# Expert down weights loaded as neighbouring rows, with a stepped product on VectorE to match

## The chip, the cores and the metric

The kernel runs on one core of a Trainium2 chip. The metric is the device time of one execution in microseconds (us), and a kernel's time is the median of its runs. The profile is of one further execution, taken by the hardware profiler.

## What is computed

A two-layer trunk over one sequence of 256 tokens with 1024 channels, in float32: a convolution module and a dense SwiGLU, then shared keys and values, a windowed attention and a mixture of experts, then a final norm. The change lies in the experts. The reference for them, shortened:

```python
D_FF_EXPERT, N_EXPERTS, TOP_K = 3584, 8, 2

def swiglu(t, w_gate, w_up, w_down):
    return (jax.nn.silu(t @ w_gate) * (t @ w_up)) @ w_down

def moe_swiglu(h, router_w, router_b, w_gate, w_up, w_down):
    ...
    out = jnp.zeros_like(t)
    for e in range(N_EXPERTS):
        out = out + combine[:, e:e + 1] * swiglu(t, w_gate[e], w_up[e], w_down[e])
    return out.reshape(B, S, D)
```

The product with `w_down` is a sum over the 3584 hidden channels. Any order of these channels gives the same sum, as long as the activations and the rows of `w_down` are in the same order.

## The kernel before, in words

**The expert stage.** The kernel makes one pass for each expert (and one more for each expert with over 128 tokens; here there are eight passes in all). A pass gathers up to 128 tokens of the expert and goes through the 3584 hidden channels in seven blocks of 512 (`EB`). For each block it computes the gate product, the up product and the down product, each as three float32r matmuls in place of one float32 matmul: every weight and every activation is split into a high part (`wh`, `ath`) and a low part (`wl`, `atl`), and high by high, low by high and high by low are summed in PSUM (`three_passes`, whose matmuls the profile shows at L992).

**Units and halves.** Weights come in units of 1 MB, 8 KB in each of the 128 partitions. A block has six: two each for gate, up and down (`expert_units`, line 89). A gate or up unit holds 512 columns of four rows for each partition, so pieces of 2 KB. A down unit holds two whole rows of `w_down` (1024 floats, 4 KB) for each partition; row k of a block's four row groups is at channel 128 k + p for partition p (line 454), so the two rows of one partition lie 512 KB apart. Each unit is split in two halves. ScalarE copies a half to its high part (`high_parts`, L687), VectorE subtracts it to get the low part (`low_parts`, L1428), and six matmuls of TensorE use it.

**Buffers.** The raw units lie in a ring of seven (`RING`), the split halves in four places (`SPLITS`). SP issues the load of a unit when VectorE has split the unit seven before it (line 461). ScalarE writes a high part when TensorE has used the half four before it.

**One block, in the order of each queue.** All orders are written out by hand.
- TensorE (`expert_pass`, line 1259): gate of block b, the transposes of block b-1's activations, up of block b, down of block b-1. After the last block it transposes the last activations, gathers the next pass's tokens, does the down product, and begins the next pass's gate product.
- ScalarE (line 829): the silu of the gate product into the tile `act` (L823), the high part of the transposed activations (L827), and the high halves of the weights in the order of use.
- VectorE (line 1695): low halves of the gate and up weights, the low part of the transposed activations (`act_low`, L1679), low halves of the previous block's down weights, and then `gate_up` (line 1682, the product at L1686): `act` is multiplied by the up product in PSUM bank 1. The result goes back into `act`. In block 3 of every pass `slots(i + 1)` comes right behind it (lines 1708 to 1711): it loads two registers and makes four selection tiles for the next pass (`pick_slots`, L1632 and L1636).
- TensorE's `transpose_act` (line 1240, L1243) waits for that product and turns its four chunks of 128 channels (`act[:, j * P:(j + 1) * P]`) into four stationary tiles, chunk j against row group j of the block's down weights in `expert_out`.

R3 is a float32 tile of 128x3136; `act` is its first 512 columns and appears as `R` in the profile.

Of the kernel before, what the change touches and what calls it, by code (L numbers as in the profile page):

```python
# [20 lines left out]
P = 128  # L21
# [47 lines left out]
ALU = mybir.AluOpType  # L69
# [19 lines left out]
def expert_units():  # L89

    order = [("g", 0), ("u", 0)]
    for b in range(1, EB):
        order += [("g", b), ("u", b), ("d", b - 1)]
    order.append(("d", EB - 1))
    return [(kind, b, part) for kind, b in order for part in range(2)]
# [18 lines left out]
def trunk(nc, x, norm_mix_g, norm_ffn_g, conv_pw1_w, conv_pw1_b, conv_dw_w, conv_dw_b, conv_ln_g,  # L114
# [4 lines left out]
    with ctx:  # L119
        def sb(name, shape, dt=F32):  # L120
            return ctx.enter_context(nc.sbuf_tensor(name, shape, dt))

        def sem(name):
            return ctx.enter_context(nc.semaphore(name))
# [26 lines left out]
        R3 = sb("R3", [P, 3136])  # L151
        ident = sb("ident", [P, P])
# [12 lines left out]
        PB = [ctx.enter_context(nc.psum_tensor(f"bank{b}", [P, HALF], F32)) for b in range(8)]  # L165
# [46 lines left out]
        hnh = high[:, CHUNK:CHUNK + TT * D].rearrange("p (t d) -> p t d", t=TT)  # L212
        hrT = R2[:, 0:2048].rearrange("p (k s) -> p k s", k=DC)
        act = R3[:, 0:512]
        pickg = R3[:, 1280:1536].rearrange("p (t s) -> p t s", t=TT)
        iota = R3[:, 2816:3072]
        tri = R3[:, 2368:2496]
# [117 lines left out]
        act_ready = sem("act_ready")  # L335
# [8 lines left out]
        def slot(n):  # L344
            return ring[:, n % RING, :]
# [10 lines left out]
        def product_done(eng, n, later=0):  # L356

            if n < U_FFD:
                eng.wait_ge(units_used, n + 1)
            else:  # L360
                eng.wait_ge(halves_used, later * PASS_HALVES + half_no(n, 1) + 1)
# [11 lines left out]
        def split_done(eng, n, h, later=0):  # L373

            eng.wait_ge(wl_ready, later * PASS_HALVES + half_no(n, h) + 1)
# [4 lines left out]
        def tokens(ap, t):  # L380
            return ap[..., t * P:(t + 1) * P]

        def x_bank(t, half):
            return PB[2 * t + half]
# [21 lines left out]
        def _(sp):  # L406
# [44 lines left out]

            mg = moe_w_gate[0].rearrange("e (k p) f -> e p k f", p=P)
            mu = moe_w_up[0].rearrange("e (k p) f -> e p k f", p=P)
            md = moe_w_down[0].rearrange("e (k p) f -> e p k f", p=P)

            def load_pass(i, e):

                for u, (kind, b, part) in enumerate(expert_units()):
                    n = U_MOE + u

                    split_done(sp, n - RING, 1, i)
                    if kind == "d":
                        dst = slot(n).rearrange("p (k f) -> p k f", k=2)
                        src = md[bass.ds(e, 1), :, 4 * b + 2 * part:4 * b + 2 * part + 2, :]
                    else:
                        dst = slot(n).rearrange("p (k f) -> p k f", k=4)
                        src = (mg if kind == "g" else mu)[bass.ds(e, 1), :, 4 * part:4 * part + 4,
                                                          HALF * b:HALF * (b + 1)]
                    sp.dma_start(dst, src.rearrange("e p k f -> p (e k) f")).then_inc(slot_in[n % RING], 16)


            load_pass(0, 0)
            with sp.Fori(1, E) as e:
                load_pass(e, e)
# [3 lines left out]
            with sp.If(passes > E):  # L478
                with sp.Fori(E, passes) as i:
                    e = sp.value_load(tab[0:1, bass.ds(i, 1)], min_val=0, max_val=E - 1)  # L480
                    load_pass(i, e)
# [397 lines left out]
        def _(pe):  # L879
# [34 lines left out]
            for c in range(DC):  # L914
                mm = pe.transpose(PB[3][:, 32 * c:32 * c + CONV], rows[32:32 + CONV, c * P:(c + 1) * P],
                                  ident[32:32 + CONV, 32:32 + CONV])
# [3 lines left out]
            for j in range(4):  # L920
# [4 lines left out]
                for g in range(2):  # L925
# [6 lines left out]
                    for c in range(2):  # L932
                        for k in range(DC):
                            if n == 0 and c == 0:
                                h_ready(0, k)
                            mm = pe.matmul(PB[2 * g + j % 2][:, c * S:(c + 1) * S], w[:, k, c * P:(c + 1) * P],  # L936
                                           hT[:, k, :], start=(k == 0), stop=(k == DC - 1))
# [12 lines left out]
            for m, (c, w) in enumerate(matrix_taps()):  # L950

                pe.wait_ge(tap_act, m + 1)
                if w == 0:
                    pe.wait_ge(glu_ready, c + 1)
                last_tap = SHARED_TAPS - 1 if c == DVE_CHUNKS else CONV - 1
                mm = pe.matmul(PB[4 + c - DVE_CHUNKS][:, 0:S], taps[:, m % DIAGS, :], upad[:, c, w:w + S],  # L956
                               start=(w == 0), stop=(w == last_tap))
# [6 lines left out]
            for t in range(TT):  # L964
                for c in range(DC):
                    pe.wait_ge(sq_ready, 2 * t + (1 if c < DVE_CHUNKS else 2))
                    mm = pe.matmul(PB[3 - t][:, 0:P], ones[:, :], tokens(sq[:, c, :], t), start=(c == 0),  # L967
                                   stop=(c == DC - 1))
# [3 lines left out]
            for t in range(TT):  # L972
                for k in range(DC):
# [4 lines left out]
                    for half in range(2):  # L978
                        mm = pe.matmul(x_bank(t, half)[:, :], tokens(sq[:, k, :], t),  # L979
                                       w[:, k % 2, half * HALF:(half + 1) * HALF], start=(k == 0),  # L980
                                       stop=(k == DC - 1))
# [7 lines left out]
            def three_passes(out_bank, a, b, start, stop, **kw):  # L989

                for n, (lhs, rhs) in enumerate(((a[0], b[0]), (a[1], b[0]), (a[0], b[1]))):
                    mm = pe.matmul(out_bank, lhs, rhs, start=start and n == 0, stop=stop and n == 2, **kw)  # L992
                return mm

            def parts(n, h, cols):

                return wh[:, place(n, h), cols], wl[:, place(n, h), cols]
# [76 lines left out]
            for t in range(TT):  # L1074
                for k in range(DC):
                    if t == 0 and k % 4 == 0:
                        split_done(pe, U_KV + 1, k // 4)
                    mm = three_passes(PB[1][:, t * S:(t + 1) * S], (tokens(hTh[:, k, :], t), tokens(hTl[:, k, :], t)),
                                      parts(U_KV + 1, k // 4, slice(k % 4 * S, (k % 4 + 1) * S)),
                                      k == 0, k == DC - 1)  # L1080
# [79 lines left out]
            for t in range(TT):  # L1160

                pe.wait_ge(x_upd, B_X + 2 * (t + 1))
                for k in range(DC):
                    mm = pe.transpose(PB[4 + 2 * t + k // 4][:, k % 4 * P:(k % 4 + 1) * P], X[:, t, k * P:(k + 1) * P],
                                      ident[:, :])
# [4 lines left out]
            for t in range(TT):  # L1170
                pe.wait_ge(hrT_act, t + 1)
                pe.wait_ge(hrT_dve, t + 1)
                for k in range(DC):
                    mm = pe.matmul(PB[t][:, 0:E], hrT[:, k, t * P:(t + 1) * P], rw[:, k, :],
                                   start=(k == 0), stop=(k == DC - 1))
# [64 lines left out]
            def transpose_act(i, b):  # L1240
                pe.wait_ge(act_ready, i * EB + (b + 1))
                for j in range(4):
                    mm = pe.transpose(PB[2][:, j * P:(j + 1) * P], act[:, j * P:(j + 1) * P], ident[:, :])  # L1243
                mm.then_inc(actT_done, 1)

            def combine(i, t, banks=(5, 6)):
# [12 lines left out]
            def expert_pass(i, last):  # L1259

                pe.wait_ge(gates_ready, i + 1)
                for t in range(TT):

                    pe.matmul(PB[7][:, S:S + 1], pickg[:, t, :], ones[:, 0:1], start=(t == 0), stop=(t == TT - 1))
                for t in range(TT):
                    mm = pe.transpose(PB[7][:, t * P:(t + 1) * P], pick[:, t, :].bitcast(F32), ident[:, :])
                mm.then_inc(place_done, 1)
                for b in range(1, EB):
                    expert_in(i, "g", b)
                    transpose_act(i, b - 1)  # L1270
                    expert_in(i, "u", b)
                    expert_out(i, b - 1)
                transpose_act(i, EB - 1)
                gather(i + 1)
                expert_out(i, EB - 1, (0,))
                gather_T(i + 1)
                expert_out(i, EB - 1, (1,))

                if not last:
                    expert_in(i + 1, "g", 0)  # L1280
                combine(i, 0)
                if not last:
                    expert_in(i + 1, "u", 0)
                    combine(i, 1)
                else:
                    combine(i, 1, (0, 1))
# [19 lines left out]
        def _(ve):  # L1306
# [375 lines left out]
            def gate_up(i, b):  # L1682

                ve.wait_ge(sil_ready, i * EB + (b + 1))
                product_done(ve, expert_at["u", b, 1], i)
                ve.tensor_tensor(act, PB[1][:, :], act, ALU.mult).then_inc(act_ready, 1)  # L1686

            def add_share(i, t, banks=(5, 6)):

# [5 lines left out]
            def expert_pass(i, last):  # L1695

                gate_up(i, 0)
                split_low(i, "u", 1)
                act_low(i, 0)
                split_low(i, "d", 0)  # L1700
                gate_up(i, 1)
                for b in range(2, EB):
                    split_low(i, "g", b)
                    split_low(i, "u", b)
                    act_low(i, b - 1)
                    split_low(i, "d", b - 1)
                    gate_up(i, b)
                    if b == 3:

                        ve.wait_ge(place_done, i + 1)  # L1710
                        slots(i + 1)
# [81 lines left out]
```

## Time and profile before

| | |
|---|---|
| median of 3 runs | 1433.01 us (1430.46 to 1433.05) |
| the profiled execution: its time | 1430.62 us |
| its span, from the first to the last instruction | 1428.9 us |
| TensorE (PE) busy | 1406.5 us, 98% |
| VectorE (DVE) busy | 1170.0 us, 82% |
| ScalarE (ACT) busy | 990.4 us, 69% |
| GpSimd (POOL) busy | 35.8 us, 3% |
| granted TensorE clock | 0.997 of full speed |
| moved by DMA | 417.47 MB, 292 GB/s over the span |

Busy times of one engine are shares of the same span, so they don't add up over engines. PEld is TensorE's weight load, which runs beside its matmuls. A matmul's end is modelled: two that follow each other overlap in the profile, so their pace is read from their starts or from the chain. The idle time of an engine that isn't the bottleneck costs nothing by itself.

### The profile page before, as it was taken

How to read it: one execution, taken by the hardware profiler on the slowest of the kernel's cores; microseconds unless marked ns; L12 is line 12 of the kernel's file. 1: busy time of each engine (PE TensorE's matmuls, PEld its weight loads, DVE VectorE, ACT ScalarE, POOL GpSimd, SP SyncE). 2: the span in 40 equal slices, each digit the busy share in tenths (PEclk: the TensorE clock that was granted, in tenths of full speed). 3: DMA queues.
4: the chain of work that ended last, by engine and by line, in shares of the span. 5: the costliest groups of instructions: out<-in, count | busy, mean ns of one | idle time of the engine just before them, and what ended most of it. 6: DMA issues, size and time to landing. Idle time of an engine off the chain costs nothing.

```text
span 1428.9 us, 21427 instructions
## 1 busy us (share of the span) xinstructions
PE 1406.5 (98%) x7251; PEld 1185.9 (83%) x7251; DVE 1170.0 (82%) x1340; ACT 990.4 (69%) x1224; POOL 35.8 (3%) x62
## 2 busy tenths in 40 slices
PE   9999999999999999999999999999999999999997
PEld 8885999998887888888888888888888888888885
DVE  3983454456769998998999899899989989999996
ACT  2174434445657888887888888787888888878775
POOL 1000000002220000000000000000000000000000
PEclk9999999999999999999999999999999999999999
DMA  9602655655528999999999899999989999998991
GB/s 293 209 28 91 204 177 182 197 181 177 178 89 295 366 381 322 373 360 345 359 363 380 313 382 360 342 363 366 382 311 377 366 328 369 356 390 319 373 364 76
DMA packets 194063, 417.47 MB, mean 292 GB/s; under 512 B 6911, under 2 KB 43903, under 8 KB 194014
## 3 DMA queue, kind: packets, MB, share of 16 engines
q1 hardware_dynamic: 192510, 412.79, 80.6%
q0 software_dynamic: 1344, 3.98, 1.2%
q8 instruction: 31, 0.51, 0.1%
q14 instruction: 18, 0.15, 0.0%
q10 hardware_dynamic: 160, 0.04, 0.0%
HBM read 414.95 MB, written 1.84 MB: 292 GB/s over the span
## 4 chain that ended last, share of the span: by engine, by line
PE 94%; DVE 2%; ACT 2%; issue 1%; POOL 1%; DMA 0%; DVEq 0%; POOLq 0%; ACTq 0%
PE bank L992 78%; PE bank L936 4%; PE bank L956 2%; PE bank L979 2%; PE bank L1243 2%; PE bank L891 1%; PE bank L1194 1%; PE bank L1255 1%; DVE wl L1428 1%; ACT wh L687 1%; PE bank L903 0%; ACT low L812 0%; POOL prob L567 0%; PE bank L1205 0%; PE bank L967 0%
## 5 line engine op out<-in xcount | busy, mean ns | idle before, releaser
L1428 DVE TENSOR_TENSOR wl<-ring,wh 128x1024 fp32r<-128x1024 f32 x758 | 905.8, 1221 | 115.1 <-ACT wh L687 75.8
L687 ACT CAST wh<-ring 128x1024 fp32r<-128x1024 f32 x758 | 787.8, 1054 | 187.7 <-PE bank L992 187.6
L992 PE MATMUL bank<-wh,low 128*128 128x512 f32 (+1 forms) x1840 | 576.1, 392 | 3.4 <-DVE wl L1428 2.8
L992 PEld LDWEIGHTS bank<-wh,low 128*128 128x128 f32 x1840 | 339.6, 188 | 75.9 <-DVE wl L1428 8.7
L992 PE MATMUL bank<-wl,low 128*128 128x512 f32 x896 | 349.7, 390 | 0.0
L992 PE MATMUL bank<-wh,ath 128*128 128x512 f32 x528 | 206.3, 391 | 0.0
L992 PE MATMUL bank<-wh,atl 128*128 128x512 f32 x528 | 205.6, 389 | 0.0
L992 PE MATMUL bank<-wl,ath 128*128 128x512 f32 x528 | 205.5, 389 | 0.0
L992 PEld LDWEIGHTS bank<-wl,low 128*128 128x128 f32 x896 | 168.2, 188 | 36.0
L992 PEld LDWEIGHTS bank<-wl,ath 128*128 128x128 f32 x528 | 99.1, 188 | 20.8
L992 PEld LDWEIGHTS bank<-wh,ath 128*128 128x128 f32 x528 | 99.2, 188 | 20.2
L992 PEld LDWEIGHTS bank<-wh,atl 128*128 128x128 f32 x528 | 99.2, 188 | 19.9
L992 PE MATMUL bank<-high,wh 128*128 128x256 f32 x368 | 104.3, 283 | 0.7 <-DVE low L1439 0.7
L992 PE MATMUL bank<-low,wh 128*128 128x256 f32 x368 | 104.1, 283 | 0.0
L992 PE MATMUL bank<-high,wl 128*128 128x256 f32 x368 | 104.1, 283 | 0.0
L992 PEld LDWEIGHTS bank<-high,wh 128*128 128x128 f32 x368 | 70.6, 192 | 1.4 <-DVE low L1439 0.7
L992 PEld LDWEIGHTS bank<-high,wl 128*128 128x128 f32 x368 | 70.6, 192 | 0.4
L992 PEld LDWEIGHTS bank<-low,wh 128*128 128x128 f32 x368 | 70.6, 192 | 0.0
L1377 DVE SCALAR_TENSOR_TENSOR R<-R 128x256 f32<-128x256 f32 x169 | 67.4, 476 | 0.0
L936 PE MATMUL bank<-R,ring 128*128 128x256 f32 x256 | 55.5, 379 | 0.0
L936 PEld LDWEIGHTS bank<-R,ring 128*128 128x128 f32 x256 | 48.6, 190 | 6.9 <-issue 0.3
L1679 DVE TENSOR_TENSOR atl<-bank,ath 128x512 fp32r<-128x512 f32 x56 | 38.3, 684 | 10.5 <-ACT ath L827 10.5
(213 smaller groups left out, 998.8 us busy)
## 6 DMA issues: line engine op xcount, KB each, us to landing
ring<-in_moe_w_gate SPq DMA_DIRECT2D x112, 1024.0 KB, 5.9
ring<-in_moe_w_up SPq DMA_DIRECT2D x112, 1024.0 KB, 6.3
ring<-in_moe_w_down SPq DMA_DIRECT2D x112, 1024.0 KB, 6.3
ring<-in_conv_pw_w SPq DMA_DIRECT2D x12, 1024.0 KB, 11.2
ring<-in_ffd_w_gate SPq DMA_DIRECT2D x11, 1024.0 KB, 5.4
ring<-in_ffd_w_up SPq DMA_DIRECT2D x11, 1024.0 KB, 5.3
ring<-in_ffd_w_down SPq DMA_DIRECT2D x11, 1024.0 KB, 4.9
ring<-in_w_q SPq DMA_DIRECT2D x4, 1024.0 KB, 4.9
```

The source lines that it names most:

```text
L687: sa.copy(wh[:, place(n, h), :], ring_half(n, h)).then_inc(wh_ready, 1)
L891: pe.matmul(PB[bank][:, 0:P], ident[:, :], ident[:, :], start=True, stop=True)
L936: mm = pe.matmul(PB[2 * g + j % 2][:, c * S:(c + 1) * S], w[:, k, c * P:(c + 1) * P], hT[:, k, :], start=(k == 0), stop=(k == DC - 1))
L956: mm = pe.matmul(PB[4 + c - DVE_CHUNKS][:, 0:S], taps[:, m % DIAGS, :], upad[:, c, w:w + S], start=(w == 0), stop=(w == last_tap))
L979: mm = pe.matmul(x_bank(t, half)[:, :], tokens(sq[:, k, :], t), w[:, k % 2, half * HALF:(half + 1) * HALF], start=(k == 0), stop=(k == DC ...
L992: mm = pe.matmul(out_bank, lhs, rhs, start=start and n == 0, stop=stop and n == 2, **kw)
L1194: mm = pe.matmul(PB[5 + half][:, :], pick[:, t, :], part[:, t, half * HALF:(half + 1) * HALF], start=(t == 0 and n == 0), stop=(t == 1 and ...
L1243: mm = pe.transpose(PB[2][:, j * P:(j + 1) * P], act[:, j * P:(j + 1) * P], ident[:, :])
L1255: mm = pe.matmul(PB[banks[half]][:, :], placeT[:, t * P:(t + 1) * P], part[:, half * HALF:(half + 1) * HALF], start=(n == 0), stop=(n == 1))
L1377: ins = ve.scalar_tensor_tensor(out=v, in0=upad[:, c, w:w + S], scalar=dw[:, c, w:w + 1], in1=v, op0=ALU.mult, op1=ALU.add)
L1428: ve.tensor_tensor(wl[:, place(n, h), :], ring_half(n, h), wh[:, place(n, h), :].bitcast(F32), ALU.subtract).then_inc(wl_ready, 1)
L1679: ve.tensor_tensor(atl[:, :, :], PB[2][:, :].rearrange("p (j s) -> p j s", j=4), ath[:, :, :].bitcast(F32), ALU.subtract).then_inc(atl_rea ...
```

## The change

The load of a down unit views the down weights of a block as channel 4 p + k for partition p and row group k. The four rows of one partition are then neighbours in memory, 16 KB in one piece, and a unit takes half of them, 8 KB in one piece. To match, the activation of channel 4 q + j has to be element q of chunk j. VectorE's product puts it there: it reads both inputs with a step of four floats and writes each chunk in a row, into a new tile `act_by`, columns 512 to 1023 of R3. The transposes read `act_by`.

```diff
         act = R3[:, 0:512]
+        act_by = R3[:, 512:1024]
...
-            md = moe_w_down[0].rearrange("e (k p) f -> e p k f", p=P)
+            md = moe_w_down[0].rearrange("e (b p k) f -> e p b k f", p=P, k=4)
...
-                        src = md[bass.ds(e, 1), :, 4 * b + 2 * part:4 * b + 2 * part + 2, :]
+                        src = md[bass.ds(e, 1), :, b, 2 * part:2 * part + 2, :]
...
-                    mm = pe.transpose(PB[2][:, j * P:(j + 1) * P], act[:, j * P:(j + 1) * P], ident[:, :])
+                    mm = pe.transpose(PB[2][:, j * P:(j + 1) * P], act_by[:, j * P:(j + 1) * P], ident[:, :])
...
-                ve.tensor_tensor(act, PB[1][:, :], act, ALU.mult).then_inc(act_ready, 1)
+                ve.tensor_tensor(act_by.rearrange("p (j q) -> p j q", j=4),
+                                 PB[1][:, :].rearrange("p (q j) -> p j q", j=4),
+                                 act.rearrange("p (q j) -> p j q", j=4), ALU.mult).then_inc(act_ready, 1)
```

## Rows read from the trace of the kernel before

**Rows 1.** The page: busy time by engine, and the chain that ended last.
```profile
PE 1406.5 (98%) x7251; PEld 1185.9 (83%) x7251; DVE 1170.0 (82%) x1340; ACT 990.4 (69%) x1224; POOL 35.8 (3%) x62
...
PE 94%; DVE 2%; ACT 2%; issue 1%; POOL 1%; DMA 0%; DVEq 0%; POOLq 0%; ACTq 0%
```

**Rows 2.** Stretches: start:end and length, busy by engine, clock, DMA share, GB/s.
```profile
813.00:936.30 123.30, 123.10 (x563) 101.53 (x563) 114.14 (x111) 99.85 (x109) 0.00 (x0) 1.00 0.98 357
...
sum 976.30, PE 973.28 PEld 802.53 DVE 900.75 ACT 783.81 POOL 0.00; mean PE 121.66 PEld 100.32 DVE 112.59 ACT 97.98 POOL 0.00
```

**Rows 3.** Waits from 480 to 1420 us: total us, times, longest.
```profile
ACT wh L687 <- PE bank L992: 154.3, 487, 1.9
DVE wl L1428 <- ACT wh L687: 22.4, 29, 2.1
...
PEld bank L992 <- DVE wl L1428: 6.8, 20, 0.6
```

**Rows 4.** The chain in order of time: start, length, what.
```profile
835.95 16.38 PE bank L992 x72
...
885.97 0.44 PE bank L1243 x4
...
914.13 0.44 PE bank L1243 x4
```

**Rows 5.** The last pass: a stretch, and the chain.
```profile
1409.00:1414.00 5.00, 5.00 (x28) 4.21 (x27) 2.90 (x4) 3.78 (x6) 0.00 (x0) 1.00 0.00 0
...
1410.07 2.75 PE bank L992 x12
```

**Rows 6.** DMA issues with us to landing; all ring landings, 600 to 1300; SP's waits.
```profile
ring<-in_moe_w_gate SPq DMA_DIRECT2D x112, 1024.0 KB, 5.9
...
ring<-in_moe_w_down SPq DMA_DIRECT2D x112, 1024.0 KB, 6.3
...
DMA to landing us min/median/max: 4.8/6.2/8.1
...
SPq L469 <- DVE wl L1428: 850.0, 336, 21.7
```

**Rows 7.** Groups of VectorE instructions: count, busy us, mean ns, idle before.
```profile
L1428 DVE TENSOR_TENSOR wl<-ring,wh 128x1024 fp32r<-128x1024 f32 x758 | 905.8, 1221 | 115.1 <-ACT wh L687 75.8
...
L1686 DVE TENSOR_TENSOR R<-bank,R 128x512 f32<-128x512 f32 x56 | 38.2, 682 | 0.4 <-issue 0.4
...
L1415 DVE RECIPROCAL R<-R 128x128 f32<-128x128 f32 x2 | 1.9, 950 | 1.9 <-ACT R L666 1.9
```

**Rows 8.** Timeline, VectorE and TensorE around a product: start, us, instruction, count.
```profile
877.36 0.68 DVE L1686 TENSOR_TENSOR R<-bank,R 128x512 f32<-128x512 f32 x1
877.96 1.22 DVE L1428 TENSOR_TENSOR wl<-ring,wh 128x1024 fp32r<-128x1024 f32 x1
...
880.37 0.61 PE L992 MATMUL bank<-wh,low 128*128 128x512 f32 x2
...
910.96 0.68 DVE L1686 TENSOR_TENSOR R<-bank,R 128x512 f32<-128x512 f32 x1
911.56 2.35 DVE L1428 TENSOR_TENSOR wl<-ring,wh 128x1024 fp32r<-128x1024 f32 x2
```

**Rows 9.** Timeline around block 3 of a pass, and the like waits elsewhere.
```profile
860.50 0.68 DVE L1686 TENSOR_TENSOR R<-bank,R 128x512 f32<-128x512 f32 x1
861.24 0.48 DVE L1632 TENSOR_SCALAR pick<-R,small 128x128 fp32r x2
...
862.15 1.22 DVE L1428 TENSOR_TENSOR wl<-ring,wh 128x1024 fp32r<-128x1024 f32 x1
...
863.42 0.30 PEld L992 LDWEIGHTS bank<-wh,low 128*128 128x128 f32 x2 [0.18 <-DVE wl L1428]
...
493.40 0.30 PEld L992 LDWEIGHTS bank<-wh,low 128*128 128x128 f32 x2 [0.19 <-DVE wl L1428]
...
1357.09 0.30 PEld L992 LDWEIGHTS bank<-wh,low 128*128 128x128 f32 x2 [0.48 <-DVE wl L1428]
```

## The prediction

> **What bounds the kernel now.** I read the page first: TensorE is busy for 98% of the span and holds 94% of the chain that ended last [rows 1]. So I asked which engine the others wait for in the expert stage, the only part that the change touches: 976.3 us from its first pass to its last, two thirds of the span [rows 2]. One whole pass (one expert, seven blocks of 512 hidden columns) has TensorE busy for 123.1 of 123.3 us at full clock, VectorE for 114.1, ScalarE for 99.9, and the DMA engines at a share of 0.98 [rows 2]. The waits say who leads: ScalarE waits for TensorE to free a split buffer, 154.3 us in all, TensorE waits for VectorE's low halves (L1428) only 6.8 us, and no row of this stretch names a DMA [rows 3]. The chain of one block is 72 matmuls in 16.38 us and four transposes in 0.44 us, 16.82 us a block [rows 4], or 227 ns a matmul. In the last pass, with no DMA running, 12 matmuls take 2.75 us, 229 ns each [rows 5]. So the traffic doesn't slow the matmuls, and lighter traffic can't quicken them. The expert stage is TensorE's own pace, plus the few places where VectorE is late.
>
> **Parts that cost nothing.** The change adds and removes no instruction, semaphore or DMA. The four transposes of a block read another tile of the same form (0.44 us as before), and the hidden rows are summed in another order. SP issues the same two 1 MB loads a block for the down weights, each in 8 KB pieces where it had two pieces of 4 KB for a partition. The gate loads come in 2 KB pieces and land in 5.9 us, the down loads in 4 KB pieces and land in 6.3 [rows 6]: doubling the piece brought nothing that can be seen, so I take 6.3 us again. What covers it: a block needs six units, so a unit is used every 16.82/6 = 2.8 us and a ring of seven holds 19.6 us of work; even the slowest landing, 8.1 us, leaves over 8 us after the first split of a unit and the engines' lead over TensorE (about 3 us) are taken off. SP sat 850.0 us waiting for VectorE to free slots, at every one of the 336 units [rows 6]; it is never the late one. Gain or loss: 0. The cover is gone only if loads fall behind for good (below).
>
> **The part that can cost: VectorE's product (L1686).** It is one instruction a block, 56 in all, 682 ns each now [rows 7]. After the change both inputs (PSUM bank 1, and the silu result in SBUF) are read with a step of four floats, 16 bytes, and written in a row. Nothing in this trace reads or writes in such steps, so its price is bounded. From below: a product of 1024 elements takes 1221 ns and one of 512 takes 682, so VectorE moves an element in (1221-682)/512 = 1.05 ns on a fixed 145 ns, and a step may cost nothing: 682 ns. From above: the costliest element of any VectorE row is the reciprocal's, 950 ns for 128, or 6.3 ns each, which would make 3.4 us of it [rows 7]; that is its arithmetic, though, and no read. Between them I take one more turn of the engine for each element, that is the row of twice the elements, 1221 ns, and d = 0.54 us extra. Of these ends the value is much the nearer to 682; a gain I exclude, since no tensor_tensor row moves an element faster than 1.05 ns.
>
> Beside this, the Trainium skill ("Vector Engine (DVE) Microarchitecture Reference", section 5.2, the access granule) speaks against the change. It says that a port streams at full rate only if elements come as runs of two or more adjacent 4-byte words, and lists 1.75 ns a column for both SBUF sources stepping 72 or 152 words, 2.5 for steps of 24, against 1.05 in a row. No run here shows a stepped read; the row-wise rate agrees with this trace's 1.05. By it d would be 0.36 to 0.74 us and the sum +1.7 to +4.8 us. It lists neither a step of four words nor a PSUM source.
>
> **Where d lands.** Usually in slack. In an ordinary block the product starts at 877.36 and the next low half at 877.96, ending at 877.96 + 1.22 = 879.18; TensorE wants it at 880.37 [rows 8]. So 1.19 us of lateness are free there. When VectorE is behind, two low halves take 2.35 us and so start 1.13 apart [rows 8], while TensorE eats one in six matmuls, 1.36 us: it regains 0.2 us with each, and a block has 12. The transposes that need the product come at 885.97, 7.9 us after its end, and in the last block at 914.13 after 910.96 + 0.68 = 911.64, still 2.5 us [rows 4, 8].
>
> Block 3 of each pass is different. There four small VectorE operations that pick the next expert's tokens (L1632, L1636) stand right behind the product: it starts at 860.50, they run from 861.24, the next low half starts at 862.15 and ends at 863.37, and TensorE loads its weights at 863.42 after waiting 0.18 us for it [rows 9]. The slack is used up; every extra VectorE nanosecond in this place is one of TensorE. Such a wait stands in each of the eight passes, from 493.40 to 1357.09, the last one 0.48 us [rows 9]. One part comes back. The pick starts 0.74 us after the product, where a low half follows in 0.60 [rows 8, 9]: the queue is still working out the pick's addresses, and a longer product hides these 0.14 us. TensorE's other waits for VectorE stand at the ends of passes, where VectorE itself waits for ScalarE's splits (22.4 us in all [rows 3]) and not behind the product.
>
> The sum: 8 x (0.54 - 0.14) = +3.2 us. On the profiled execution's span, 1428.9 becomes 1432.1, its time 1430.6 becomes 1433.8. The median of the three runs is 1433.0, 2.4 above that execution, so the forecast in their measure is 1433.0 + 3.2 = 1436.2.
>
> **Rivals.**
> 1. *The step is free.* For it: every VectorE row goes by element count alone, whatever the source. Against it: no row has a step of more than one inside a run. Then d = 0, nothing else in the change reaches TensorE, and the time stays 1433.0: not slower. The Trainium skill ("SBUF — State Buffer", the note on cachelines) bears on it: it puts the free step at 4 fp32, just this one, though it also asks for two hits in a line of 16 bytes, which this step doesn't give. No row here decides it.
> 2. *The step costs two more turns or more* (one for each source, say). With 683 + 2 x 538 = 1.76 us, d = 1.08 stays under the 1.19 us of the ordinary blocks and costs 8 x (1.08 - 0.14) = 7.5 us: 1440.5. From d = 1.19 on, the other blocks stall as well and it goes up fast: with d = 1.6, 8 x 1.46 + 48 x 0.41 = 31 us, 1464. Against it: that far from every row.
> 3. *The 8 KB pieces are slower to fetch.* They lie 16 KB apart from partition to partition, where the 4 KB pieces lay side by side over all 128. The DMA share of 0.98 says there is little reserve: if down loads take over some 6% longer (a third of the bytes, so 2% of the whole), the ring runs dry and each further per cent of the expert stage costs 9.8 us. A down load a quarter slower gives (8 - 2)% of 976 us, +59 us: 1492. Against it: 2 KB and 4 KB pieces land alike [rows 6].
> 4. *Faster.* Larger pieces lighten the DMA engines. It would have to reach TensorE, which has the same pace with no traffic at all [rows 5] and waits for no transfer [rows 3]. I see no mechanism; 1430 is what the spread of the runs gives.
>
> **How the numbers follow.** A measurement of this kernel can tell about 0.2%, 2.9 us, from no change. Chances: the forecast 0.56, the free step 0.30, more turns 0.05, slow pieces 0.04, faster 0.05. The forecast's own bounds, from d a little above the 0.14 that is hidden to d = 0.75, are +1.5 to +4.9 us, and 2.9 lies near their middle: 0.33 of its 0.56 falls above 0.2%, 0.23 below. With the two dear rivals and the odd high run that makes slower 0.43; with the free step, same 0.51; faster 0.06. The range holds the first two cases: 1430.5, where the free step meets the lowest run seen, to 1436.2 + 1.7 for the upper bound + 1 for the spread of the medians, 1439. The dear rivals are left out.
>
> **What would show it.** The product's mean in the groups by line: 682 ns (rival 1), near 1.2 us (forecast), over 1.75 (rival 2). TensorE's wait for the low half in block 3: 0.18 us (rival 1), near 0.6 (forecast), and the passes 123.7 us where they were 123.3. Waits for VectorE in other blocks mean rival 2; waits of ScalarE for the DMA and a landing well over 6.3 us for the down loads mean rival 3. The forecast is wrong if the product lengthens and the block 3 wait doesn't, or if the passes change and the product doesn't.

## The result

| | before | changed | ratio |
|---|---|---|---|
| median of 20 runs each | 1431.38 us (1430.01 to 1433.34) | 1433.03 us (1431.71 to 1434.84) | 1.0013 (95%: 1.0007 to 1.0018) |
| the profiled execution: time, span | 1430.62, 1428.9 us | 1433.02, 1431.3 us | |

The changed kernel is 1.65 us slower, inside the 0.2% that I called no change, though the ratio's interval excludes 1. The ratio is estimated, with its interval, from the single runs and needn't be the quotient of the two medians. The 1433.0 from which the forecast was counted came from three runs; twenty put the kernel before at 1431.4.

### The profile after

The page of the changed kernel (the diff adds a line, so L1686 is now L1687, L1428 is L1429, L992 is L993):

```profile
PE 1408.3 (98%) x7251; PEld 1185.9 (83%) x7251; DVE 1184.5 (83%) x1340; ACT 990.5 (69%) x1224; POOL 35.7 (2%) x62
...
L1687 DVE TENSOR_TENSOR R<-bank,R 128x512 f32<-128x512 f32 x56 | 59.8, 1069 | 0.4 <-issue 0.4
...
ring<-in_moe_w_down SPq DMA_DIRECT2D x112, 1024.0 KB, 7.0
```

The product went from 682 ns [rows 7] to 1069. VectorE's timeline in block 3 of the pass that [rows 9] shows of before, and the weight load that waits for it:

```profile
861.80 1.07 DVE L1687 TENSOR_TENSOR R<-bank,R 128x512 f32<-128x512 f32 x1
862.78 0.48 DVE L1633 TENSOR_SCALAR pick<-R,small 128x128 fp32r x2
863.17 0.60 DVE L1637 TENSOR_SCALAR R<-R,small 128x128 f32 x2
863.68 3.49 DVE L1429 TENSOR_TENSOR wl<-ring,wh 128x1024 fp32r<-128x1024 f32 x3
...
864.96 0.30 PEld L993 LDWEIGHTS bank<-wh,low 128*128 128x128 f32 x2 [0.41 <-DVE wl L1429]
```

From the product's start to the low half it was 862.15 - 860.50 = 1.65 us and is 863.68 - 861.80 = 1.88. The product grew by 0.39 and the low half is 0.23 later: the pick now starts 0.98 us after the product's start where it was 0.74, so some 0.15 us of the longer product were hidden in the queue, as forecast. TensorE's weight load waits 0.41 us where it waited 0.18.

How that adds up, by the starts of the first and the last pass on TensorE. First before, then after:

```profile
442.34 0.60 PE L1264 MATMUL bank<-ones,R 128*128 128x1 f32 x4
...
1305.83 0.50 PE L1264 MATMUL bank<-ones,R 128*128 128x1 f32 x4
```

```profile
442.79 0.57 PE L1265 MATMUL bank<-ones,R 128*128 128x1 f32 x4
...
1308.23 0.50 PE L1265 MATMUL bank<-ones,R 128*128 128x1 f32 x4
```

Seven passes took 863.49 us and take 865.44: 123.36 and 123.63 us each, +0.28 us a pass and +1.95 us in all. From its start to the end of the span the last pass takes 123.03 us in both. The other 0.45 us of the span were there before the first pass, where no product of the change has run yet.

### The profile page after: what moved, and what is told of

The parts are those of the page before. It is cut to its first block, busy times and chain, and to the rows that moved or that the text cites. A ratio compares the mean times of both kernels' runs of the same rounds, so it can differ in the third digit from the quotient of the medians.

```text
span 1431.3 us, 21427 instructions
## 1 busy us (share of the span) xinstructions
PE 1408.3 (98%) x7251; PEld 1185.9 (83%) x7251; DVE 1184.5 (83%) x1340; ACT 990.5 (69%) x1224; POOL 35.7 (2%) x62
## 4 chain that ended last, share of the span: by engine, by line
PE 94%; ACT 2%; DVE 2%; issue 1%; DMA 0%; ACTq 0%; DVEq 0%; POOL 0%; POOLq 0%
PE bank L993 79%; PE bank L937 4%; PE bank L957 2%; PE bank L980 2%; PE bank L1244 2%; PE bank L1195 1%; PE bank L1256 1%; DVE wl L1429 1%; ACT wh L688 1%; PE bank L892 1%; PE bank L904 0%; DMA R<-in_conv_ln_b 0%; ACT low L813 0%; PE bank L1206 0%; PE bank L1175 0%
## 5 line engine op out<-in xcount | busy, mean ns | idle before, releaser
L1429 DVE TENSOR_TENSOR wl<-ring,wh 128x1024 fp32r<-128x1024 f32 x758 | 899.5, 1220 | 106.2 <-ACT wh L688 74.1
L993 PE MATMUL bank<-wh,low 128*128 128x512 f32 (+1 forms) x1840 | 577.0, 393 | 3.4 <-DVE wl L1429 2.8
L993 PEld LDWEIGHTS bank<-wh,low 128*128 128x128 f32 x1840 | 339.6, 188 | 77.8 <-DVE wl L1429 10.2
L993 PE MATMUL bank<-wl,low 128*128 128x512 f32 x896 | 349.7, 390 | 0.0
L993 PE MATMUL bank<-wh,ath 128*128 128x512 f32 x528 | 206.3, 391 | 0.0
L993 PE MATMUL bank<-wh,atl 128*128 128x512 f32 x528 | 205.6, 389 | 0.0
L993 PE MATMUL bank<-wl,ath 128*128 128x512 f32 x528 | 205.5, 389 | 0.0
L993 PEld LDWEIGHTS bank<-wl,low 128*128 128x128 f32 x896 | 168.1, 188 | 36.1
L993 PEld LDWEIGHTS bank<-wl,ath 128*128 128x128 f32 x528 | 99.1, 188 | 20.8
L993 PEld LDWEIGHTS bank<-wh,ath 128*128 128x128 f32 x528 | 99.1, 188 | 20.3
L993 PEld LDWEIGHTS bank<-wh,atl 128*128 128x128 f32 x528 | 99.2, 188 | 19.8
L993 PE MATMUL bank<-high,wh 128*128 128x256 f32 x368 | 104.3, 283 | 0.7 <-DVE low L1440 0.7
L993 PE MATMUL bank<-low,wh 128*128 128x256 f32 x368 | 104.1, 283 | 0.0
L993 PE MATMUL bank<-high,wl 128*128 128x256 f32 x368 | 104.1, 283 | 0.0
L993 PEld LDWEIGHTS bank<-high,wh 128*128 128x128 f32 x368 | 70.6, 192 | 1.4 <-DVE low L1440 0.7
L993 PEld LDWEIGHTS bank<-high,wl 128*128 128x128 f32 x368 | 70.6, 192 | 0.4
L993 PEld LDWEIGHTS bank<-low,wh 128*128 128x128 f32 x368 | 70.6, 192 | 0.0
L1687 DVE TENSOR_TENSOR R<-bank,R 128x512 f32<-128x512 f32 x56 | 59.8, 1069 | 0.4 <-issue 0.4
```

Source lines behind the costliest of these rows:

```text
L1429: ve.tensor_tensor(wl[:, place(n, h), :], ring_half(n, h), wh[:, place(n, h), :].bitcast(F32), ALU.subtract).then_inc(wl_ready, 1)
L1687: ve.tensor_tensor(act_by.rearrange("p (j q) -> p j q", j=4), PB[1][:, :].rearrange("p (q j) -> p j q", j=4), act.rearrange("p (q j) -> p ...
```

## The experiments

Theory A is the mechanism of the forecast: the stepped product makes one low half late, in block 3. Theory B is the first rival to it after the result, since the landing times had grown: the 8 KB pieces cost.

### 1. Each half of the change alone, and the small operations moved

`e1_load_only` is the kernel before with the two changed lines of the loads:

```diff
-            md = moe_w_down[0].rearrange("e (k p) f -> e p k f", p=P)
+            md = moe_w_down[0].rearrange("e (b p k) f -> e p b k f", p=P, k=4)
...
-                        src = md[bass.ds(e, 1), :, 4 * b + 2 * part:4 * b + 2 * part + 2, :]
+                        src = md[bass.ds(e, 1), :, b, 2 * part:2 * part + 2, :]
```

> Only the loads of the change: 8 KB pieces, the product and the transposes as before. It sums the hidden activations against down rows in another order, so what it computes is another sum of the same size; no work is left out. Theory A (the stepped product behind block 3 is the whole cost): no change against before, ratio 1.000, product 682 ns, block 3 waits 0.18 us. Theory B (the 8 KB pieces cost, landings went from 6.2 to 7.3 us): +1.7 us, ratio 1.0012, and the landings at 7.3 us. Under A the landings may still be 7.3.

`e2_step_only` is the changed kernel with these two lines taken back.

> Only the stepped product and the new tile, with the loads of before in 4 KB pieces. The activations meet down rows in another order, so it too computes another sum; no work is left out. Theory A: product 1067 ns, block 3 waits 0.42 us in seven passes and 0.48 in the last, +1.7 us, ratio 1.0012. Theory B: ratio 1.000 although the product is longer; landings back at 6.2 us.

`e3_after_slots` is the changed kernel with this, and `e4_before_slots` the kernel before with the same:

```diff
                 for b in range(2, EB):
                     split_low(i, "g", b)
+                    if b == 4:
+
+                        ve.wait_ge(place_done, i + 1)
+                        slots(i + 1)
                     split_low(i, "u", b)
                     act_low(i, b - 1)
                     split_low(i, "d", b - 1)
                     gate_up(i, b)
-                    if b == 3:
-
-                        ve.wait_ge(place_done, i + 1)
-                        slots(i + 1)
```

> The whole change, and the four small operations that pick the next expert's tokens moved four low halves later on VectorE, from right behind the product of block 3 to between the gate and up halves of block 4. Theory A: the product's 0.39 us and the 1 us of the small operations are each under the 1.19 us that are free, so the eight waits in block 3 go: 7 x 0.42 + 0.48 = 3.4 us less than the changed kernel, 1.7 less than before, ratio 0.9988. Rival: the two latenesses still add up, because VectorE regains only 0.2 us a half, and a wait of some tenths is left a few halves later: ratio about 1.000.

> The kernel before with the same move of the small operations. Theory A: 7 x 0.18 + 0.48 = 1.7 us less than before, ratio 0.9988, so equal to the changed kernel with the move: with the slack restored the stepped product is free. Rival (the step costs something elsewhere too): this one is faster than the changed kernel with the move by up to 1.7 us.

| run | ratio to before (95%) | median, before beside it | down landing, us |
|---|---|---|---|
| loads alone | 0.9992 (0.9982 to 1.0002) | 1431.20, 1431.24 | 6.3 |
| stepped product alone | 1.0014 (1.0003 to 1.0026) | 1433.91, 1431.24 | 6.6 |
| changed, operations moved | 0.9989 (0.9978 to 1.0000) | 1430.45, 1431.24 | 6.9 |
| before, operations moved | 0.9989 (0.9977 to 1.0001) | 1429.79, 1431.24 | 5.2 |

One pass of each as a stretch (columns as in [rows 2]), first the loads alone, then the stepped product alone, then the changed kernel with the move, then before with the move.

```profile
813.10:936.40 123.30, 123.10 (x563) 101.53 (x562) 114.13 (x111) 99.84 (x109) 0.00 (x0) 1.00 0.98 357
```
```profile
813.80:937.40 123.60, 123.39 (x564) 101.55 (x563) 115.98 (x111) 99.89 (x109) 0.00 (x0) 1.00 0.97 356
```
```profile
813.40:936.70 123.30, 123.10 (x564) 101.67 (x563) 115.73 (x111) 99.92 (x109) 0.00 (x0) 1.00 0.97 358
```
```profile
812.20:935.50 123.30, 123.10 (x564) 101.67 (x563) 114.00 (x111) 99.90 (x109) 0.00 (x0) 1.00 0.98 357
```

Theory B falls: the loads alone leave the pass at 123.30 us. The step alone, with the old 4 KB pieces, gives the whole 123.60. And with the small operations out of the way the step is free: VectorE is nearly as busy as with the step alone (115.73 us of the pass beside 115.98), and the pass is back at 123.30. All seven passes say the same, by their starts as above: 863.61 us with the loads alone, 865.48 with the step alone, 863.25 and 863.18 for the changed kernel and the kernel before with the move. The waits agree. The stretch from 480 to 1420 us, loads alone:

```profile
PEld bank L992 <- DVE wl L1428: 6.0, 15, 0.6
```

and with both the step and the move:

```profile
PEld bank L993 <- DVE wl L1429: 4.5, 8, 0.6
```

which are the pass ends alone. What I expected of the move was too much, though. Of its 3.4 us on the changed kernel the medians give some 2.6 (1433.03 against 1430.45, from two sessions), and so does the profile: 2.19 in seven passes and 0.37 in the last, which goes from 123.03 to 122.66 us. On the kernel before the profile gives 0.31 us in seven passes (863.49 to 863.18) and 0.35 in the last, 0.66 in all where I expected 1.7. The wait of 0.18 us that I read in block 3 was almost free, then, at under 0.05 us a pass: it is the weight load that waits, and it begins before its matmul is due.

### 2. Which port pays for the step

`e5_psum_step` steps only through PSUM, `e6_sbuf_step` only through SBUF:

```diff
                                  PB[1][:, :].rearrange("p (q j) -> p j q", j=4),
-                                 act.rearrange("p (q j) -> p j q", j=4), ALU.mult).then_inc(act_ready, 1)
+                                 act.rearrange("p (j q) -> p j q", j=4), ALU.mult).then_inc(act_ready, 1)
```
```diff
-                                 PB[1][:, :].rearrange("p (q j) -> p j q", j=4),
+                                 PB[1][:, :].rearrange("p (j q) -> p j q", j=4),
                                  act.rearrange("p (q j) -> p j q", j=4), ALU.mult).then_inc(act_ready, 1)
```

> The whole change, but only the up product in PSUM is read with the step of four floats; the silu result in SBUF is read in a row, so pairs that don't belong together are multiplied and the result is another one. Theory P (one stepped source costs as much as two): 1.05 to 1.07 us. Theory Q (the step costs nothing in PSUM, all of the 0.39 us comes from the SBUF source): 683 ns, and block 3 back at 0.18 us. Theory R (each source adds its half): 875 ns.

> The same with only the silu result in SBUF read with the step, the PSUM product in a row; again other pairs are multiplied. Theories P and Q: 1.05 to 1.07 us, with block 3 at 0.42 us. Theory R: 875 ns.

The product in the groups by line, PSUM alone, then SBUF alone:

```profile
L1687 DVE TENSOR_TENSOR R<-bank,R 128x512 f32<-128x512 f32 x56 | 38.3, 684 | 0.4 <-issue 0.4
```
```profile
L1687 DVE TENSOR_TENSOR R<-bank,R 128x512 f32<-128x512 f32 x56 | 60.0, 1071 | 0.4 <-issue 0.4
```

Theory Q: in this product a step of 16 bytes through PSUM costs VectorE nothing, the same step through SBUF costs (1071 - 684)/512 = 0.76 ns an element, and stepping both costs no more than that. Each of the two ran once (1431.63 and 1431.74 us), so their times tell nothing; the stage of the profile does. With PSUM alone block 3 waits at most 0.19 us in the first seven passes, which take 863.58 us together; with SBUF alone it waits 0.41 to 0.43 us and they take 865.46.

`e7_write_step` reads both sources in a row and writes with a step of 128 floats:

```diff
-                ve.tensor_tensor(act_by.rearrange("p (j q) -> p j q", j=4),
-                                 PB[1][:, :].rearrange("p (q j) -> p j q", j=4),
-                                 act.rearrange("p (q j) -> p j q", j=4), ALU.mult).then_inc(act_ready, 1)
+                ve.tensor_tensor(act_by.rearrange("p (j q) -> p q j", j=4),
+                                 PB[1][:, :].rearrange("p (q j) -> p q j", j=4),
+                                 act.rearrange("p (q j) -> p q j", j=4), ALU.mult).then_inc(act_ready, 1)
```

> The whole change with the step on the other side: VectorE reads both sources in a row and writes each element 128 floats (512 bytes) from the last; the result tile is the same. Theory P for the write too: 1.02 to 1.07 us and the time of the changed kernel, ratio to before 1.0013. Rival: a step on the write costs more, 1.4 us (two more turns for each element or nearly), then block 3 waits 0.8 us and the ratio is 1.003.

It took 1097 ns and the ratio was 1.0017 (1.0007 to 1.0026); the median was 1432.66 us beside 1431.03. VectorE's timeline in block 3:

```profile
861.31 1.10 DVE L1687 TENSOR_TENSOR R<-bank,R 128x512 f32<-128x512 f32 x1
862.24 0.46 DVE L1633 TENSOR_SCALAR pick<-R,small 128x128 fp32r x2
...
863.13 3.49 DVE L1429 TENSOR_TENSOR wl<-ring,wh 128x1024 fp32r<-128x1024 f32 x3
...
864.40 0.30 PEld L993 LDWEIGHTS bank<-wh,low 128*128 128x128 f32 x2 [0.34 <-DVE wl L1429]
```

A stepped write costs about the same in duration, but the pick starts 0.93 us after the product's start, 0.05 sooner than with the stepped read, and TensorE's wait is 0.34 us. The seven passes take 864.75 us, 0.7 less than the changed kernel's, which the medians are too coarse to show.

`e8_transpose_step` has the loads of the change and gives the step to TensorE:

```diff
+            act_q = act.rearrange("p (q j) -> p j q", j=4)
+
             def transpose_act(i, b):
                 pe.wait_ge(act_ready, i * EB + (b + 1))
                 for j in range(4):
-                    mm = pe.transpose(PB[2][:, j * P:(j + 1) * P], act[:, j * P:(j + 1) * P], ident[:, :])
+                    mm = pe.transpose(PB[2][:, j * P:(j + 1) * P], act_q[:, j, :], ident[:, :])
```

> The loads of the change with the product as before (682 ns, in a row); TensorE's four transposes of a block read their 128 columns with the step of four floats instead. Theory A: nothing on VectorE gets longer, block 3 waits 0.18 us. If a stepped stationary tile is free for TensorE, the time is that of before, ratio 0.9995 to 1.000. Rival: the load of a stepped tile (139 ns in a row) takes up to twice as long and isn't hidden between the short matmuls, 4 x 0.07 to 4 x 0.14 us in each of 56 blocks, +16 to +31 us, ratio 1.011 to 1.022.

The ratio was 1.0015 (1.0006 to 1.0024), 1433.30 us beside 1431.03, between the two expectations. The load of the stationary tile took 205 ns where it took 140:

```profile
L1245 PEld LDWEIGHTS bank<-ident,R 128*128 128x128 f32 x224 | 35.8, 205 | 4.0
```

and the chain, with the four transposes between blocks at 0.47 us where they were 0.44 [rows 4]:

```profile
838.55 0.47 PE bank L1245 x4
839.03 16.36 PE bank L992 x72
```

Four loads that each take 65 ns longer show as only 0.03 us in the chain, so nearly all of it is hidden beside the matmuls. The rest, 0.03 us x 56 = 1.7 us, lies on the path in every block; by the pass starts it is 1.76 us in seven passes and 0.26 in the last.

### 3. How much lateness the other blocks take

`e9_two_more` and `e10_three_more` put two and three useless products ahead of each real one in the kernel before (with `range(3)` in the second):

```diff
+                for n in range(2):
+                    ve.tensor_tensor(R1[:, n * HALF:(n + 1) * HALF], PB[1][:, :], act, ALU.mult)
                 ve.tensor_tensor(act, PB[1][:, :], act, ALU.mult).then_inc(act_ready, 1)
```

> The kernel before with two further products of the same size ahead of each real one on VectorE, into columns of R1 that nothing reads: every product is late by 2 x 0.60 = 1.20 us, about the slack of 1.19 us read in an ordinary block. Theory A (only what follows block 3 is exposed): the waits there are about 0.18 + 1.2 - 0.14 = 1.2 us, the passes about 1.1 us longer, +8 to +9 us in all, ratio 1.006; in the other blocks no wait, or one of under 0.1 us. Rival (the slack of ordinary blocks is smaller than it was read): waits in all seven blocks, over +20 us, ratio above 1.014.

> The same with three further products, 1.81 us late in every block. Theory A: over the slack everywhere, about 1.81 - 1.19 = 0.6 us in each ordinary block beside 1.7 us in block 3, and VectorE, which regains about 2.7 us in a block and is asked for 1.35 + 1.81, falls behind by some 0.4 us a block for good: +30 us (20 to 45), ratio 1.014 to 1.031. Rival (the cost grows in proportion, with no threshold): one and a half times that of the kernel with two, +13 us, ratio 1.009.

Measured: 1450.69 us beside 1431.18, ratio 1.0138 (1.0123 to 1.0154), and 1481.82, ratio 1.0357 (1.0341 to 1.0373). Both are above what I expected; the first is close to its rival, by which the slack is smaller than I read it. Weight loads that waited for VectorE in blocks 0 to 3 of the pass from 820 us of `e9_two_more`:

```profile
826.75 0.30 PEld L992 LDWEIGHTS bank<-wh,low 128*128 128x128 f32 x2 [0.34 <-DVE wl L1428]
838.23 0.30 PEld L992 LDWEIGHTS bank<-wh,low 128*128 128x128 f32 x2 [0.70 <-DVE wl L1428]
855.27 0.30 PEld L992 LDWEIGHTS bank<-wh,low 128*128 128x128 f32 x2 [0.32 <-DVE wl L1428]
873.16 0.30 PEld L992 LDWEIGHTS bank<-wh,low 128*128 128x128 f32 x2 [1.22 <-DVE wl L1428]
```

Block 3 (at 873.16) is as expected, 1.22 us. The others should have had none; blocks 4 and 5 wait 0.32 us as block 2 does, and only block 6 has no such wait. The free lateness of an ordinary block was misread: I took it up to the matmul at 880.37, but its weight load comes first. From the trace of before:

```profile
880.14 0.41 PEld L992 LDWEIGHTS bank<-wh,low 128*128 128x128 f32 x2
```

So 880.14 - 879.18 = 0.96 us are free, not 1.19. The run itself says a little less: 1.20 us of lateness leave a wait of 0.32, so 0.88 are free. The waits for VectorE from 480 to 1420 us with three more:

```profile
PEld bank L992 <- DVE wl L1428: 52.3, 53, 1.8
PE bank L992 <- DVE wl L1428: 32.0, 50, 1.4
```

Half as much lateness again cost two and a half times as much, 50.6 us against 19.5. There is a threshold, then, and the 0.39 us of the change are well under it. The trace with three more also says where the 50.6 us lie. VectorE in block 5 of a pass, and the one weight load that waits for it in blocks 4 and 5:

```profile
1043.45 5.22 DVE L1428 TENSOR_TENSOR wl<-ring,wh 128x1024 fp32r<-128x1024 f32 x4
1048.58 1.88 DVE L1687 TENSOR_TENSOR R<-bank,R 128x512 f32<-128x512 f32 x3
...
1034.67 0.30 PEld L992 LDWEIGHTS bank<-wh,low 128*128 128x128 f32 x2 [0.92 <-DVE wl L1428]
...
1052.25 0.30 PEld L992 LDWEIGHTS bank<-wh,low 128*128 128x128 f32 x2 [0.91 <-DVE wl L1428]
```

The low halves ahead of the products start (5.22 - 1.22)/3 = 1.33 us apart, about the 1.36 of TensorE's six matmuls and not the 1.13 of a VectorE that is behind: it has caught up by then. So it doesn't fall behind for good, which I had expected. The third product's 0.60 us adds to the wait behind the products, 0.32 to 0.92 us, in each block whose slack the first two had used up.

### 4. The order of channels without a stepped SBUF access

Since PSUM can be read with a step for nothing, `e11_silu_order` lets both PSUM reads do it. It is the changed kernel with:

```diff
-                sa.activation(act, PB[0][:, :], ACT.Silu).then_inc(sil_ready, 1)
+                sa.activation(act.rearrange("p (j q) -> p j q", j=4),
+                              PB[0][:, :].rearrange("p (q j) -> p j q", j=4), ACT.Silu).then_inc(sil_ready, 1)
...
-                                 act.rearrange("p (q j) -> p j q", j=4), ALU.mult).then_inc(act_ready, 1)
+                                 act.rearrange("p (j q) -> p j q", j=4), ALU.mult).then_inc(act_ready, 1)
```

> The loads of the change, with no stepped read or write of SBUF: ScalarE's silu reads its PSUM bank with the step of four floats and writes the chunks in a row, and VectorE's product reads PSUM with the step (free on VectorE by the run with the PSUM step alone) and the silu in a row. Theory A: product 683 ns, block 3 waits 0.18 us, the time of the run with the loads alone, ratio to before 0.999 to 1.000. Rival: a stepped PSUM read costs ScalarE a second turn an element, 602 ns becomes some 1.03 us; then the next high half is 0.4 us later, which ScalarE's wait for TensorE of 0.3 us a half takes up in two halves, and the ratio is still under 1.001.

`e12_silu_order_slots` has the move of the small operations as well.

> The same, with the four small operations moved to block 4 as before. Theory A: no wait for VectorE but those at the ends of passes, the time of the kernel before with that move, ratio 0.9989. Rival: the step on ScalarE costs something in its place, ratio about 1.000.

The silu and the product of `e11_silu_order`, and seven passes as one stretch:

```profile
L824 ACT ACTIVATE R<-bank 128x512 f32<-128x512 f32 x56 | 33.6, 600 | 0.1
...
L1688 DVE TENSOR_TENSOR R<-bank,R 128x512 f32<-128x512 f32 x56 | 38.3, 684 | 0.4 <-issue 0.4
...
444.50:1308.10 863.60, 862.19 (x3935) 711.15 (x3935) 799.40 (x770) 698.86 (x755) 0.00 (x0) 1.00 0.98 358
```

The stepped PSUM read is free on ScalarE too (602 ns before), and the seven passes take 863.6 us, as before. Yet the ratio over the runs was 1.0010 (1.0001 to 1.0019), 1432.80 us beside 1431.18, so the expectation of the time was missed. In the profiled execution the extra lies ahead of the first pass, which begins at 444.50 us where it began at 442.34. With the move the ratio was 0.9992 (0.9983 to 1.0001), 1430.47 us, near what I expected; its first pass began at 441.87, and TensorE waits for VectorE no more in block 3. The later start arises in the routing stage ahead of the passes, whose chain has 4.14 us at L1176 where it was 3.47 before (L1174) and 4.89 at L893 where it was 4.19 (L891). Whether it comes with the kernel or by chance was not settled, so what `e11_silu_order` costs in whole time stays open.

No version is clearly faster than the kernel before. The three with the move have intervals whose upper ends are 1.0000 or 1.0001; the two of them whose product is not lengthened (`e4_before_slots`, `e12_silu_order_slots`) have the shortest profiled spans, 1428.1 and 1427.8 us.

## Why the prediction came out as it did

**What bounds the kernel: right.** The chain is still 94% TensorE, and the DMA still waits for VectorE at all 336 units (854.4 us in all, 850.0 before [rows 6]).

**The loads cost nothing: right**, by the run with the loads alone. The term "6.3 us again" came out as 7.0 and the cover held, as it should by the working. But this landing time says nothing of the pieces: the gate loads, which the change leaves alone, went from 5.9 to 7.2 us in the same execution, and the down loads landed in 6.3 us with 8 KB pieces alone, 6.6 with 4 KB pieces and the step, and 5.2 in an execution of the kernel before with the operations moved.

**The step costs time on VectorE: right, the size too large.** The term d was 0.54 us, one more turn for each element, and is 0.39. The figure of the Trainium skill ("Vector Engine (DVE) Microarchitecture Reference", section 5.2) for steps of 72 or 152 words, 1.75 ns a column, gave 0.36; this trace has 0.76 + 1.05 = 1.81 ns, so it agrees with that row and not with the 2.5 ns for 24 words, though in that row both sources are in SBUF and here one is. The other page of the Trainium skill ("SBUF — State Buffer", the note on cachelines) puts the free step at 4 fp32; that doesn't hold here for SBUF (1071 ns with the SBUF source stepping, 684 without), while its condition of two hits in a line of 16 bytes, which this step doesn't give, goes with the cost. PSUM, which section 5.2 doesn't list, is free at this step. Rival 1, the free step, is refuted by the product's 1069 ns. That its 1433.0 is also the measured median is luck: the base was 1.6 us lower than three runs had said, and the change cost 1.65. Its argument, that every VectorE row goes by element count alone, was also read too widely: the reciprocal's 950 ns for 128 elements stands beside it in [rows 7].

**It lands behind block 3 alone, less the 0.14 us: right for seven passes.** The 0.54 - 0.14 = 0.40 a pass became a low half 0.23 us later and a pass 0.28 longer; where the other 0.05 us arise wasn't traced. What failed in this step is the factor 8. In the last pass, which runs from another copy of the loop, the queue was late by itself. VectorE's timeline there before and after:

```profile
1353.86 0.68 DVE L1686 TENSOR_TENSOR R<-bank,R 128x512 f32<-128x512 f32 x1
1354.61 0.48 DVE L1632 TENSOR_SCALAR pick<-R,small 128x128 fp32r x2
1355.30 0.60 DVE L1636 TENSOR_SCALAR R<-R,small 128x128 f32 x2 [0.20 <-issue]
1355.81 1.22 DVE L1428 TENSOR_TENSOR wl<-ring,wh 128x1024 fp32r<-128x1024 f32 x1
```
```profile
1356.26 1.07 DVE L1687 TENSOR_TENSOR R<-bank,R 128x512 f32<-128x512 f32 x1
...
1357.69 0.60 DVE L1637 TENSOR_SCALAR R<-R,small 128x128 f32 x2
1358.21 1.22 DVE L1429 TENSOR_TENSOR wl<-ring,wh 128x1024 fp32r<-128x1024 f32 x1
```

From the product's start to the low half it is 1.95 us in both, and the second pair of small operations (L1636, then L1637) starts 1.44 and 1.43 us after it: here the queue sets the time, and it takes up all 0.39 us of the longer product, 0.25 more than the 0.14 forecast, and TensorE waits 0.48 us as before. Why the queue is later in this pass is not shown. The 0.48 us wait in [rows 9] was the hint, and I counted that pass like the others.

**The sum.** +3.2 us was 8 x 0.40; it is 7 x 0.28 = 1.95 in the profile and 1.65 in the medians. The size of d is the larger error: 0.28 for 0.40 us a pass takes off 1.0 us, the factor 7 for 8 another 0.3. Both corrections go the same way and take the sum from just over the 0.2% to under it. Of the 3.2 us between the forecast 1436.2 and the measured 1433.03, the base makes up 1.6 us and the size of the term the rest. So the range held with the mechanism right and its size too large. The slack of the ordinary blocks (1.19 us, really 0.96) was wrong without consequence; rival 2 would have come sooner than I put it.

## What to carry to other kernels

Before making loads more regular, ask whether anything waits for them: here SP waited for slots at every unit, so larger pieces had nothing to give. A reordering by such a step in float32 is best put on the read of a PSUM bank, where 16 bytes were free on two engines, and not on an SBUF read or write. The price of a slower instruction is set where the queue has the least slack, in this kernel one place in seven blocks; count slack up to the weight load and not to its matmul, and look at the last round of a loop by itself.

## What was unexpected of the hardware

- A VectorE product with one SBUF source stepping 16 bytes takes 1071 ns for 512 floats, 684 ns if only the PSUM source steps, and 1069 ns if both do; a write stepping 512 bytes makes it 1097. ScalarE's silu reads PSUM with the step in 600 ns (602 in a row). A stepped stationary tile of 128 columns loads in 205 ns instead of 140.
- The first seven passes agree within 0.15 us in the profiled execution before (123.32 to 123.47 us) and after (123.56 to 123.71), and their sum in two kernels with the same product and order within about 0.1, while the medians move by one or two: the start of the first pass ranged from 441.51 to 444.64 us over profiled executions of kernels whose stages ahead of it are the same. Differences of a tenth of a per cent are better read from the stage than from the whole time.
